# Spreading decay and gate rows over the partitions: one float32r product of high and low parts instead of float32 products, and a narrow product ahead of two more units

## The reference, cut to what matters

```
c = jnp.cumsum(log_f, axis=-1)
logits = q @ k.T * scale + cq[..., :, None] - c[..., None, :]
```

```
gc = jnp.cumsum(gc, axis=-1)
decay = exp(gc[..., :, None] - gc[..., None, :])
m = strict(kb @ k.T * decay)        # kb = k * beta
q_dec = qc * jnp.exp(gc)[..., None]
```

## Time and profile before

| | us |
|---|---|
| three runs: median (lowest to highest) | 2060.71 (2058.79 to 2062.12) |
| the profiled execution's own time | 2059.68 |
| its span, first to last instruction | 2057.9 |
| PE busy | 2004.3 (97%), 16645 products |
| POOL busy | 1500.7 (73%) |
| DVE busy | 866.8 (42%) |
| ACT busy | 1074.8 (52%) |
| mean granted clock of TensorE | 0.997 of full speed |

### The profile page before, as it was taken

How to read it: one execution, slowest core, us unless ns; L and a number is a source line. 1 busy time by engine, 2 the same in 40 slices (tenths; PEclk the granted TensorE clock), 3 DMA queues, 4 the chain that set the end, 5 groups by cost and what they waited for, 6 DMA issues and landing times.

```text
span 2057.9 us, 38626 instructions
## 1 busy us (share of the span) xinstructions
PE 2004.3 (97%) x16645; PEld 1863.2 (91%) x16645; DVE 866.8 (42%) x1482; ACT 1074.8 (52%) x1537; POOL 1500.7 (73%) x630
## 2 busy tenths in 40 slices
PE   7999998999998999999999999999999999999998
PEld 6888997888988999999999899989999999998998
DVE  5443237356446558465112311255484751132112
ACT  5555555555556654266445544475532664445444
POOL 6679988679976645466778788865454677787886
PEclk9999999999999999999999999999999999999999
DMA  8435553435553423235445455543232444455553
GB/s 343 150 141 205 191 189 140 149 129 198 186 174 124 144 83 128 100 127 181 146 165 201 164 195 195 194 144 125 103 124 97 151 162 155 163 196 168 198 187 133
DMA packets 47193, 331.84 MB, mean 161 GB/s; under 512 B 5168, under 2 KB 5552, under 8 KB 8112
## 3 DMA queue, kind: packets, MB, share of 16 engines
q1 hardware_dynamic: 47024, 329.38, 46.1%
HBM read 328.31 MB, written 1.05 MB: 160 GB/s over the span
## 4 chain that ended last, share of the span: by engine, by line
PE 66%; DVE 2%; ACT 1%; issue 0%; POOL 0%; DVEq 0%; ACTq 0%
PE bank L146 16%; PE bank L148 15%; PE bank L147 15%; PE y L148 3%; PE y L147 3%; PE y L146 3%; PE bank L2012 1%; PE bank L2024 1%; PE bank L2022 1%; PE bank L2071 1%; PE bank L2055 1%; PE bank L1852 1%; PE bank L2067 1%; POOL w_lo L354 0%; PE bank L1953 0%
## 5 line engine op out<-in xcount | busy, mean ns | idle before, releaser
L354 POOL TENSOR_TENSOR w_lo<-w_raw,w_hi 128x1024 fp32r<-128x1024 f32 x600 | 1466.7, 2454 | 542.6 <-ACT w_hi L345 542.0
L345 ACT ACTIVATE w_hi<-w_raw 128x1024 fp32r<-128x1024 f32 x600 | 635.2, 1061 | 845.4 <-PE bank L148 697.5
L146 PE MATMUL bank<-x_hi,w_hi 128*128 128x256 f32 x2944 | 846.2, 287 | 27.8 <-POOL w_lo L354 17.6
L148 PE MATMUL bank<-x_hi,w_lo 128*128 128x256 f32 x2944 | 820.0, 279 | 0.0
L147 PE MATMUL bank<-x_lo,w_hi 128*128 128x256 f32 x2944 | 819.9, 278 | 0.0
L146 PEld LDWEIGHTS bank<-x_hi,w_hi 128*128 128x128 f32 x2944 | 556.8, 189 | 48.8 <-issue 23.8
L147 PEld LDWEIGHTS bank<-x_lo,w_hi 128*128 128x128 f32 x2944 | 557.3, 189 | 5.1 <-issue 4.8
L148 PEld LDWEIGHTS bank<-x_hi,w_lo 128*128 128x128 f32 x2944 | 557.1, 189 | 0.0
L889 DVE SCALAR_TENSOR_TENSOR conv<-bank,par_sb,conv 128x254 f32<-128x254 f32 (+1 forms) x176 | 76.8, 478 | 205.4 <-ACT conv L877 203.8
L1491 DVE TENSOR_TENSOR hid_lo<-hid,hid_hi 128x512 fp32r<-128x512 f32 x22 | 45.0, 2046 | 235.1 <-ACT hid_hi L1486 235.1
L146 PE MATMUL y<-w_hi,hid_hi 128*128 128x512 f32 x352 | 137.6, 391 | 3.9 <-DVE hid_lo L911 2.6
(11 more groups left out here) (424 smaller groups left out, 2990.6 us busy)
## 6 DMA issues: line engine op xcount, KB each, us to landing
w_raw<-w SPq DMA_DIRECT2D x298, 1024.0 KB, 4.8
ln_rows<-ln_rows SPq DMA_DIRECT2D x4, 1024.0 KB, 7.5
w_raw<-w SPq DMA_DIRECT2D x4, 512.0 KB, 3.5
mem_tok<-mem SPq DMA_DIRECT2D x2, 1024.0 KB, 5.0
const_sb<-const SPq DMA_DIRECT2D x1, 1536.0 KB, 8.2
par_sb<-par SPq DMA_DIRECT2D x2, 553.5 KB, 10.9
xn<-xT SPq DMA_DIRECT2D x1, 1024.0 KB, 4.8
x_tok<-x SPq DMA_DIRECT2D x1, 1024.0 KB, 6.8
```

The lines of the kernel that those rows point to most:

```text
L146: pe.matmul(out, lhs[0], rhs[0], start=start, stop=False, skip_group_check=skip)
L148: return pe.matmul(out, lhs[1], rhs[0], start=False, stop=stop, skip_group_check=skip)
L345: act.activation(self.hi[:, h % HALVES, :], self.raw[:, n % RAWS, i * HW:(i + 1) * HW], ACT.Copy).then_inc(*sig.up("high", h))
L354: pool.tensor_tensor(self.lo[:, h % HALVES, :], self.raw[:, n % RAWS, i * HW:(i + 1) * HW], self.hi[:, h % HALVES, :].bitcast(F32), ALU.su ...
```

## The change

1. The selecting constant gets 104 rows: head h is selected by row h, 32+h, 64+h and 96+h, the first two for output partitions 0 to 63, the last two for 64 to 127. It is loaded at the start into `pt1` (a DMA of its own, ahead of the one for `more`), and ACT copies it into a float32r tile `selects` once, in layer 0 of the first block, behind the logarithm of the gates.
2. The rows to be spread are written four times by DVE into a float32r tile that was set to zero: high part, low part, and both again for the upper 64 partitions. Each spread is one float32r product for each head with 104 rows and 128 columns out: with 256 columns (`negc`, exp(gc)) or 128 columns (gc and beta, where the upper rows hold the second chunks of 64 tokens, so that one product writes what two half tiles did).
3. In the second block DVE does this in a new function `split_rows`, between `turn_pair` and the first taps.
4. The units `gl01` and `v0` of both layers of the second block get the narrow product ahead of them.

```diff
@@ Stream.pe
-                if part == 0 and j == 0 and u.ready is None and h and isinstance(self.halves[h - 1][2].layout, tuple):
+                if part == 0 and j == 0 and u.ready is None and h and (
+                        isinstance(self.halves[h - 1][2].layout, tuple) or u.narrow):
                     pe.matmul(u.out[:, 0:P], u.x[0][:, 0, 0:P], u.x[0][:, 0, 0:P], start=True, stop=True)
@@ Mixer1.pe
         if l == 0:
             pe.wait_ge(*sig.at("const_loaded"))
+            pe.wait_ge(*sig.at("selects"))
         pe.wait_ge(*sig.at("negc", l))
         for h in range(4):
             mm = pe.matmul(spread[:, pair_slot(h) * 256:(pair_slot(h) + 1) * 256],
-                           K("select").rearrange("p (h m) -> p h m", h=8)[0:4, h, :], m["negc"][:, :], start=True, stop=True)
+                           net.select(h), m["negc"][0:SPLIT, :], start=True, stop=True)
@@ Mixer1.act
         act.activation(lf[:, 2, :], lf[:, 2, :], ACT.Ln, bias=1.0).then_inc(*sig.up("logged", l))
+        if l == 0:
+            act.wait_ge(*sig.at("select_loaded"))
+            act.activation(net.selects[:, :, :], m["pt1"][:, :, :], ACT.Copy).then_inc(*sig.up("selects"))
@@ Mixer1.dve
-        dve.tensor_scalar(m["negc"][:, :], y, -8.0, None, ALU.mult).then_inc(*sig.up("negc", l))
+        rows = m["negc"]
+        step(dve.memset(rows[:, :].bitcast(F32), 0.0))
+        step(dve.tensor_scalar(rows[0:4, :], y, -8.0, None, ALU.mult))
+        step(dve.scalar_tensor_tensor(rows[32:36, :], y, -8.0, rows[0:4, :].bitcast(F32), ALU.mult, ALU.subtract))
+        dve.tensor_copy(rows[64:68, :], rows[0:4, :].bitcast(F32))
+        dve.tensor_copy(rows[96:100, :], rows[32:36, :].bitcast(F32)).then_inc(*sig.up("negc", l))
@@ Mixer2
+        u["gl01"].narrow = u["v0"].narrow = True
@@ Mixer2.prepare_pe
-                mm = pe.matmul(bank[b0 + hh // 2][:, (hh % 2) * T:(hh % 2 + 1) * T], sel[0:8, 4 * hf + hh, :], rows,
+                mm = pe.matmul(bank[b0 + hh // 2][:, (hh % 2) * T:(hh % 2 + 1) * T], net.select(4 * hf + hh), rows,
                                start=True, stop=True)
...
-            chunks = rows.rearrange("p (t c i) -> p c t i", t=TT, c=2)
             for hh in range(4):
-                for c in range(2):
-                    mm = pe.matmul(bank[b][c * CH:(c + 1) * CH, hh * P:(hh + 1) * P], sel[0:8, 4 * hf + hh, c * CH:(c + 1) * CH],
-                                   chunks[:, c, :, :], start=True, stop=True)
+                mm = pe.matmul(bank[b][:, hh * P:(hh + 1) * P], net.select(4 * hf + hh), rows, start=True, stop=True)
...
-            pe.wait_ge(*sig.at("decays", l))
+            pe.wait_ge(*sig.at("rows_split", l))
@@ Mixer2.act
-        act.activation(m["ge_row"][:, :], m["rowq"][:, 1, :], ACT.Exp)
+        act.activation(m["lf2"][:, :], m["rowq"][:, 1, :], ACT.Exp)
@@ Mixer2.dve
         self.turn_pair(dve, m["ik"].unsqueeze(1), 0, bank[2][:, 0:T].unsqueeze(1), net.tables[:, 1, :], net.tables[:, 3, :])
+        self.split_rows(dve)
         main.dve(dve, self.at(9))
...
+    def split_rows(self, dve):
+        row, ge, ge_row, high, chunk_rows = m["rowq"][:, 0:2, :], m["lf2"][:, :], m["ge_row"], m["row_high"], m["chunk_rows"]
+        dve.wait_ge(*sig.at("beta", l))
+        step(dve.memset(ge_row[:, :].bitcast(F32), 0.0))
+        step(dve.memset(chunk_rows[:, :, :].bitcast(F32), 0.0))
+        step(dve.tensor_copy(ge_row[0:8, :], ge))
+        step(dve.tensor_copy(high[:, :, :], row))
+        step(dve.tensor_tensor(ge_row[32:40, :], ge, ge_row[0:8, :].bitcast(F32), ALU.subtract))
+        dve.tensor_copy(ge_row[64:72, :], ge_row[0:8, :].bitcast(F32))
+        dve.tensor_copy(ge_row[96:104, :], ge_row[32:40, :].bitcast(F32))
+        whole, part = (v.rearrange("p q (t c i) -> p q t c i", t=TT, c=2) for v in (row, high[:, :, :].bitcast(F32)))
+        for c in range(2):
+            for q in range(2):
+                there = [chunk_rows[64 * c + 32 * low:64 * c + 32 * low + 8, q, :].rearrange("p (t i) -> p t i", t=TT)
+                         for low in range(2)]
+                dve.tensor_copy(there[0], part[:, q, :, c, :])
+                ins = dve.tensor_tensor(there[1], whole[:, q, :, c, :], part[:, q, :, c, :], ALU.subtract)
+        ins.then_inc(*sig.up("rows_split", l))
@@ Net.run, SP
                 main.send(sp, 5)
-                sp.dma_start(self.more[:, :], a["const"][:, NCC2:NCC]).then_inc(*sig.up("more_loaded", by=16))
+                sp.dma_start(self.mem1["pt1"][:, :, :].rearrange("p h m -> p (h m)"), a["const"][:, NCC1:NCC]
+                             ).then_inc(*sig.up("select_loaded", by=16))
+                sp.dma_start(self.more[:, :], a["const"][:, NCC2:NCC1]).then_inc(*sig.up("more_loaded", by=16))
```

More of the change, by code:

```diff
@@ L38 @@
 NEG = -1.0e30
+SPLIT = 104
 TAKEN = -3.0e38
@@ L68 @@
                      ("dn_norm", 1), ("a_log", 1), ("dt_bias", 1)])
-CC, NCC = columns([("ident", 128), ("perm64", 128), ("select", 8 * 128), ("ln_eps", 1), ("ones", 128), ("eps", 1),
+CC, NCC = columns([("ident", 128), ("perm64", 128), ("ln_eps", 1), ("ones", 128), ("eps", 1),
                    ("chunk_causal", 2 * 256), ("freq", 2), ("levels", 6 * CH), ("upper", CH),
                    ("strict", CH), ("level0T", CH), ("eye", CH),
-                   ("causal", 2 * 256), ("band", 2 * 4 * 256), ("cos", 256), ("sin", 256)])
+                   ("causal", 2 * 256), ("band", 2 * 4 * 256), ("cos", 256), ("sin", 256), ("select", 8 * 128)])
 NCC2 = CC["causal"].start
 NCC0 = CC["ones"].start
+NCC1 = CC["select"].start
 def constants():
@@ L124, in constants @@
     put("eye", (j == i).astype(np.float64))
-    sel = np.zeros((8, 8, P))
-    sel[np.arange(8), np.arange(8)] = 1.0
+    sel = np.zeros((SPLIT, 8, P))
+    for side in range(2):
+        for low in range(2):
+            sel[64 * side + 32 * low + np.arange(8), np.arange(8), side * CH:(side + 1) * CH] = 1.0
     put("select", sel)
@@ L297, in __init__ @@
         self.ready, self.act, self.dve, self.pool, self.more, self.early = ready, act, dve, pool, more, early
-        self.hooks = {}
+        self.hooks, self.narrow = {}, False
 class Stream:
@@ L1967, in prepare_pe @@
             pe.wait_ge(*sig.at("o_dn", l, 0, 1))
-        spread(m["ge_row"][:, :], 2).then_inc(*sig.up("spread_e", l, hf))
+        spread(m["ge_row"][0:SPLIT, :], 2).then_inc(*sig.up("spread_e", l, hf))
         main.pe(pe, self.step_at(hf, "k0"))
@@ L1986, in prepare_pe @@
         pe.wait_ge(*sig.at("v_read", l, hf, 1))
-        spread_chunks(m["rowq"][:, 0, :], 2).then_inc(*sig.up("spread_b", l, hf))
+        spread_chunks(m["chunk_rows"][0:SPLIT, 0, :], 2).then_inc(*sig.up("spread_b", l, hf))
         for tt in range(TT):
@@ L2445, in dve @@
         main.dve(dve, 2 * (self.units[-1].last + 1))
+    def split_rows(self, dve):
+        l, sig, m = self.l, self.net.sig, self.net.mem2
+        step = self.net.dve_chain.step
+        row, ge, ge_row, high, chunk_rows = m["rowq"][:, 0:2, :], m["lf2"][:, :], m["ge_row"], m["row_high"], m["chunk_rows"]
[15 more added lines that the diff above has]
+        ins.then_inc(*sig.up("rows_split", l))
     def prepare_dve(self, dve, hf, unit_key):
@@ L2657, in __init__ @@
         self.const = area.take("const_sb", [P, NCC2])
+        self.selects = area.take("selects", [P, 8, P], F32R)
         self.par2 = area.take("par2_sb", [P, DEPTH, NPC2])
@@ L2699, in first_memory @@
         nc = self.nc
-        self.more = area.take("const1_sb", [P, NCC - NCC2])
+        self.more = area.take("const1_sb", [P, NCC1 - NCC2])
         self.x = area.take("x_sb", [P, KD, T])
@@ L2710, in first_memory @@
         for name, shape in (("aqk", [P, 4, T]), ("bqk", [P, 4, T]), ("abv", [P, 2, 512]), ("cv", [P, 2, 256]),
-                            ("dp", [P, 2, 256]), ("cu", [P, 2, 256]), ("negc", [4, T]),
+                            ("dp", [P, 2, 256]), ("cu", [P, 2, 256]), ("negc", [P, T]),
                             ("wT", [P, 4, P]), ("cen", [P, 8, 64]), ("mean", [P, 8]), ("ms", [P, 8]),
@@ L2714, in first_memory @@
                             ("pt0", [P, 4, P]), ("pt1", [P, 8, P])):
-            m[name] = mixer.take(name, shape)
+            m[name] = mixer.take(name, shape, F32R if name == "negc" else F32)
         over = mixer.rest()
@@ L2770, in second_memory @@
         h["qw"] = place("q_and_w", 64, [P, 4, NCH, 2, CH])[:, :, :, :, :]
-        m["rowq"], m["ge_row"] = place("rowq", 72, [8, QTY - 1, T]), place("ge_row", 77, [8, T])
+        m["rowq"], m["ge_row"] = place("rowq", 72, [8, QTY - 1, T]), place("ge_row", 77, [P, T], F32R)
+        m["chunk_rows"], m["row_high"] = place("chunk_rows", 76, [P, 2, P], F32R), place("row_high", 99, [8, 2, T], F32R)
         m["cb"], m["keys"] = place("conv2", 78, [P, 2, 2, T]), place("keys", 82, [P, 4, 2, T])
@@ L2813, in repeat, with select @@
             pe.matmul(bank[:, 0:T], self.xs[0][:, 0, 0:P], self.xs[0][:, 0, :], start=True, stop=True)
+    def select(self, h):
```

(1 more changed line is left out.)

5 lines of the change are left out of this document (2 added, 3 removed).

## The result

| measured together | kernel after, us | kernel before, us | ratio |
|---|---|---|---|
| first runs | 2075.18 (2074.20 to 2076.98, 4 runs) | 2060.15 (4 runs) | 1.0073 [1.0056, 1.0091] |
| once more, with later experiments | 2076.06 (2074.55 to 2077.47, 5 runs) | 2060.76 (17 runs) | 1.0074 [1.0062, 1.0086] |

What follows compares the result with a forecast made beforehand. PE, busy 97% of the span, was taken to set the time. Savings of 6.1, 6.6 and 7.2 us against costs of 6.7, 8.3, 3.1, 0.9, 4.6 and 0.8 gave +4.5: 2065 as a median, range 2047 to 2075.

Steps and rivals of the forecast that it cites:

- The spreads: PE's spreads of gc, beta and exp(gc): 0.45 us each as float32r products, saving 6.1 and 6.6 us.
- DVE in the second block: `split_rows` held up by POOL delays q0's taps, so PE waits 6.7 and 8.3 us before the key sums.
- The clock: Half-clock stretches after PE's long waits: 2.3 us at each key sum, 4.6 together, and 0.8 in the first block.
- The first block: `negc` ready later because of DVE's added operations: +3.1 us in layer 1, +0.9 in layer 0.
- The narrow products: Ahead of gl01 and v0 they restore the stream's fast pace: 6.2 and 1.5 us, less 0.5 cost, gain 7.2.
- pace rival: Narrow products at gl01 and v0 don't restore the fast pace: +13 us, 2073; chance 0.27.

Runs made afterwards that it cites:

- e7: Kernel after with only the ten short operations of `split_rows` moved behind DVE's copies of the turned rows; 2070.93 us, ratio 1.0059 to the kernel before.
- e1: Kernel after with all of `split_rows` moved behind DVE's copies of the turned rows; 2063.34 us, ratio 1.0035 to the kernel before.
- e6: Kernel after with first block's spread as before, `split_rows` in three later parts, `o_dn_lo` later, narrow products ahead of second halves of v0 and gl01; 2046.46 us.
- e5: Kernel before with one narrow product ahead of gl01's second half in each layer; 2055.78 us, ratio 0.9976 to the kernel before.
- r_before: Kernel before, unchanged, run once more for a second trace; 2060.34 us (1 run).
- e3: Kernel before with only the narrow product ahead of gl01 added in each layer; 2060.36 us, ratio 1.0021 to the kernel before.
- e2: Kernel after with the first block's spread as in the kernel before; 2076.03 us, ratio 1.0092 to the kernel before.
- e4: Kernel after without the narrow product ahead of v0; 2079.72 us, ratio 1.0114 to the kernel before.

## Why the prediction was wrong

The forecast 2065 (+4.5) was 10 us short; the sign was right. By its own steps:

- **The spreads**: right, 0.46 for 0.45.
- **DVE in the second block**: right in mechanism and in size. Waits 7.1 and 8.7, forecast 6.7 and 8.3. e7 tells it from the rival of many small operations, e1 and e6 show that only the place makes it costly.
- **The clock**: mechanism right, a little undersized. It took 2.3 for each wait, and the half-clock stretches were 6.8 and 10.2 us long; the key sums' share is 21.2 - 15.9 = 5.3 for 4.6. The row that it started from is less firm than it looked: PE's stall of 2.8 near 642, with 3.4 us at half clock behind it in the earlier trace rows and in e5, has none behind it in r_before, e3 and e6.
- **The first block**: undersized. In layer 1 `negc` cost 4.3 with its clock (forecast 3.1 and 0.8); in layer 0 PE waited 2.4, where I took +0.9 for the whole, between the bounds, and the stream stood 2.6 later behind it. The sum is 6.8 for 4.8, or 6 against the mean of the traces with the first block of before.
- **The step that failed most is one that was left out.** The prediction counted "So gc and beta save 0.76 each" and "exp(gc) saves 1.66" as if all of it stayed with PE, with no word on who is late next; its term for waits in the second set of heads was nothing. In the second set of heads, in the kernel before, DVE finishes `e` at 792.77 + 1.61 = 794.38, 0.7 us before PE's turn of the keys at 795.13 (DVE's timeline of before, then PE's):

```profile
790.40 2.45 DVE L2598 TENSOR_TENSOR o_dn_lo<-o_turned,o_dn_hi 128x512 fp32r<-128x512 f32 x1 [0.40 <-ACT o_dn_hi L2289]
792.77 1.61 DVE L2459 TENSOR_SCALAR e<-bank,tokq 128x64 f32<-128x64 f32 x8
794.31 0.15 DVE L2468 COPY ge_last<-bank 128x8 f32<-128x8 f32 x1
```

```profile
795.13 0.60 PE L1946 MATMUL bank<-const_sb,k_set 128*128 128x128 f32 x4
```

  Two spreads ahead of it get 2.4 us shorter, so PE comes 1.7 too early if DVE's times stay where they are in the stream, as they did. After: DVE's and PE's timelines:

```profile
803.47 2.47 DVE L2631 TENSOR_TENSOR o_dn_lo<-o_turned,o_dn_hi 128x512 fp32r<-128x512 f32 x1 [0.40 <-ACT o_dn_hi L2300]
805.86 1.61 DVE L2492 TENSOR_SCALAR e<-bank,tokq 128x64 f32<-128x64 f32 x8
```

```profile
807.62 0.63 PE L1957 MATMUL bank<-const_sb,k_set 128*128 128x128 f32 x4 [1.61 <-DVE e L2492]
```

  With the wait on `ti` behind it this is 2.8 us a layer, 5.5 of the 10 missing. The rows of the kernel before were there to be read. That waiting for `e` is the cause is read from the two traces; e6, which moved `o_dn_lo` away from in front of `e`, has no wait on `e` left, though it got back only 0.7 of the 2.8.
- **The narrow products**: gl01 in the forecast's size (5.6 for 5.9), but for a wrong reason, and so by luck. It was taken to restore the fast pace; the traces show that it hands on the one it finds, and in both traces of the kernel after the stream happened to come fast. The rival's condition "if it doesn't restore" was met at v0, 1.5 us, and would have been met at gl01 too in an execution like those of e2 and e4.
- The range's upper end, 2075, was set by the pace rival, and the time lies 0.2 above it. Unnamed waits had no place in it.

Left open: what decides whether the stream arrives at gl01 at 113 or 118, and, but for the guess above, why the kernel before took 2055 beside e1 to e4 and 2060 elsewhere.

## What to carry to other kernels

- When a change shortens work on the bounding engine, read for each place behind it how long ahead the operand was ready; what exceeds that slack is no gain at that place. Here the producer's and the consumer's timelines of before give 2.4 - 0.7 = 1.7, and 1.6 was measured.
- In this kernel an operation of DVE between SBUF tiles could cost one POOL operation of 2.4 us, on 8 partitions as on 128, while POOL streamed; in a pause of POOL it took 0.2 to 0.3. So it pays to put such operations in DVE's idle gaps, a few in each, and not ahead of what another engine waits for.
- Repeats of one kernel that range over 8 us (the kernel before beside e1 to e4) hide terms of 3. A trace, compared product by product, tells a term of 0.1 at one place from nothing. Sums over a longer stretch need several traces: the first block moved by up to 1.7 us with nothing in it changed.

## What the runs showed that was not expected

- The pace of the float32r stream has two values, 113 and 118 ns for the same tiles and shapes at granted clock 1.00. A narrow product that follows 512-column products without a wait had the fast one behind it in 450 of 450 cases of the fourteen traces; behind a wait, both occurred.
- The wait of 8.7 us came with 10.2 us at granted clock 0.50, those of 7.1, 6.0 (e7) and 4.4 (e7) with 6.8; the stall of 2.8 near 642 brought 3.4 in two traces and none in three. The loss beyond the key sum's wait was 2 to 3 us in each layer.
- Four products with 104 rows and 128 columns take (694.66 - 694.26)/4 = 0.10 us each, which agrees with the earlier trace rows. The Trainium skill ("TensorE: Matmul & The Clock Gate", section "Back-to-back issue gap") gives about 81 ns for a pair with 128 columns in a stream; the float32r products of this case don't reach it.
